# Modulation rows in four column tiles, set among the x transposes and inside the first projections

## What is computed

```python
silu_c = jax.nn.silu(c)
silu_cc = jax.nn.silu(c_ctx)
for l in range(DEPTH):
    mod_l = silu_c @ w_mod[l] + b_mod[l]
    mod_c = silu_cc @ w_mod[l] + b_mod[l]
    sh_l, sc_l, g_l = jnp.split(mod_l, 3, axis=-1)
    sh_c, sc_c, g_c = jnp.split(mod_c, 3, axis=-1)
    h_l = rmsnorm(x, norm_g[l]) * (1 + sc_l[:, None]) + sh_l[:, None]
    h_c = rmsnorm(ctx, norm_g[l]) * (1 + sc_c) + sh_c
```

## Time and profile before

| | us |
|---|---|
| median of 3 runs | 3099.61 (3099.58 to 3099.64) |
| the profiled execution | 3102.97 |
| its span, first to last instruction | 3101.2 |
| TensorE busy | 2782.8 |
| VectorE busy | 1442.6 |
| ScalarE busy | 1193.2 |
| mean granted TensorE clock | 0.962 |

### The profile page before, as it was taken

How to read it: one execution, slowest core, us unless ns; L and a number is a source line. 1 busy time by engine, 2 the same in 40 slices (tenths; PEclk the granted TensorE clock), 3 DMA queues, 4 the chain that set the end, 5 groups by cost and what they waited for, 6 DMA issues and landing times. The chain is left out here.

```text
span 3101.2 us, 40301 instructions
## 1 busy us (share of the span) xinstructions
PE 2782.8 (90%) x15627; PEld 2034.4 (66%) x15627; DVE 1442.6 (47%) x2485; ACT 1193.2 (38%) x2290; POOL 141.1 (5%) x235
## 2 busy tenths in 40 slices
PE   6899999898997989998998989999898989995667
PEld 1535675466664878897776868878333877885656
DVE  1202022455554661246787552431577546348752
ACT  1400122344444342215665442221567547224542
POOL 0000000000000000000000000000000010005410
PEclk9799999999998999999999999999999999998889
DMA  7150001000000121110000222010100221010002
GB/s 283 41 185 21 16 14 43 28 1 1 1 15 21 65 72 41 42 42 29 1 2 1 96 82 82 1 55 27 41 1 21 77 77 48 28 56 27 1 34 82
DMA packets 72094, 139.44 MB, mean 45 GB/s; under 512 B 2681, under 2 KB 31762, under 8 KB 71778
## 3 DMA queue, kind: packets, MB, share of 16 engines
q1 hardware_dynamic: 59056, 92.67, 8.6%
q0 software_dynamic: 12608, 44.13, 3.9%
q10 hardware_dynamic: 242, 0.07, 0.0%
HBM read 120.08 MB, written 16.78 MB: 44 GB/s over the span
## 5 line engine op out<-in xcount | busy, mean ns | idle before, releaser
L163 ACT ACTIVATE WORK<-PS 128x512 f32<-128x512 f32 (+6 forms) x421 | 205.1, 487 | 849.2 <-PE PS L702 290.1
L163 DVE TENSOR_REDUCE SM<-PS 128x2 f32<-128x1024 f32 (+2 forms) x192 | 201.1, 1047 | 157.7 <-PE PS L986 119.3
L734 PE MATMUL PS<-BASE,WORK 128*128 128x128 f32 (+1 forms) x1278 | 198.3, 289 | 73.7 <-DVE WORK L163 57.4
L163 DVE COPY WORK<-PS 128x512 f32<-128x512 f32 (+2 forms) x135 | 84.7, 627 | 360.9 <-PEq L760 157.3
L802 PE MATMUL PS<-WORK_R,HT_R 128*128 128x512 f32 x544 | 217.7, 400 | 20.6 <-DVE W_R L163 19.6
L734 PEld LDWEIGHTS PS<-BASE,WORK 128*128 128x128 f32 (+1 forms) x1278 | 149.3, 145 | 120.4 <-DVE WORK L163 55.7
L702 PE MATMUL PS<-HT_R,W_R 128*128 128x512 f32 x576 | 225.9, 392 | 0.0
L803 PE MATMUL PS<-WORK_R,MIXT_R 128*128 128x512 f32 x544 | 215.2, 395 | 0.0
L804 PE MATMUL PS<-W_R,HT_R 128*128 128x512 f32 x544 | 214.9, 395 | 0.0
L163 ACT ACTIVATE HT<-PS 128x512 f32<-128x512 f32 (+8 forms) x232 | 125.5, 541 | 230.0 <-PE PS L734 118.7
L681 PE MATMUL PS<-HT,W 128*128 128x512 f32 (+1 forms) x576 | 209.0, 526 | 0.3 <-PE PS L681 0.3
(11 more groups left out here) (235 smaller groups left out, 5449.2 us busy)
## 6 DMA issues: line engine op xcount, KB each, us to landing
W<-in_w_mod SPq DMA_DIRECT2D x12, 2048.0 KB, 7.9
x_scratch<-WORK POOLq DMA_DIRECT2D x24, 512.0 KB, 2.9
WORK<-x_scratch POOLq DMA_DIRECT2D x24, 512.0 KB, 3.6
W<-in_odd_w_in SPq DMA_DIRECT2D x12, 1024.0 KB, 5.2
W<-in_o_w_in SPq DMA_DIRECT2D x10, 1024.0 KB, 5.3
W<-in_even_w_in SPq DMA_DIRECT2D x5, 2048.0 KB, 7.8
WORK<-in_x POOLq DMA_DIRECT2D x16, 512.0 KB, 3.9
W<-in_e_w_in SPq DMA_DIRECT2D x3, 2048.0 KB, 9.0
```

The costliest lines, as they stand in the source:

```text
L163: self.last = Signalled(self, issue(*args, **kwargs))
L734: last = nc.tensor.transpose(bank[0:m, n * P:n * P + a.shape[0]], a, IDENT[0:a.shape[0], 0:a.shape[0]])
```

## The change

- *Column tiles.* SC is widened to 32 columns for each k (two used, the others zero). Product k of a row writes partitions 32(k mod 4) to 32(k mod 4) + 31 of the bank, so four partial sums of two k each arise. VectorE copies the whole bank of 128 partitions to MROW. The four instructions that make columns are now products with MROW stationary and ROW_SUM (128 x 2, built from the identity) moving, which add the four partial sums too.
- *Order.* Of layer 0 only rows 0 to 3 (shift and scale) stand ahead of f_gate, after x tiles 3, 5, 7 and 9. Rows 4 and 5 of layer 0 and all six of layer 1 are placed behind units 4, 7, 10 of f_gate and 1, 4, 6, 8, 10 of f_in, their columns one unit later. Their weights don't pass through W: POOL loads each into one 2 MB buffer, LATE_MOD, in MIXT, the first when f_gate's first unit is done, each further one when the row before is done.
- *x tiles.* Each of the ten has its own buffer (FIRST_X) and is loaded at once; the table TABL is loaded behind them. The evictions are plain copies of a bank of 128 x 512. Scale and shift are applied afterwards in place in HT, group by group, by ScalarE (blocks 0 to 3) and VectorE (4 to 7), and f_gate waits for its group.
- *SP* starts its loads without waiting for the constants.

```diff
-        MROW = work(16384, 1024)
+        MROW = [work(16384, 512), work(16896, 512)]
+        SC = work(17408, 256).rearrange("p (k c) -> p k c", k=KT)
+        ROW_SUM = SM[:, 90:92]
+        FIRST_X = [work(o, 1024) for o in (0, 1024, 2048, 3072, 6144, 7168, 10368, 11392, 12416, 13440)]
...
-        for m in range(6):
+        for m in range(4):
             add(f"mod0_{m}", rows_by_tile(mod_w[0], 512 * m, 512 * m + 512))
         add("f_gate", rows_by_tile(e_in, 512, 1024))
-        for m in range(6):
-            add(f"mod1_{m}", rows_by_tile(mod_w[1], 512 * m, 512 * m + 512))
...
+        mod_after = {3: 0, 5: 1, 7: 2, 9: 3}
+        late_mods = [(0, 4), (0, 5)] + [(1, m) for m in range(6)]
+        late_mod_after = {("f_gate", u): n for n, u in enumerate((4, 7, 10))}
+        late_mod_after.update({("f_in", u): 3 + n for n, u in enumerate((1, 4, 6, 8, 10))})
+        LATE_MOD = MIXT[:, 4:8, :].rearrange("p k c -> p (k c)")[:, 0:WSLOT].rearrange("p (k n) -> p k n", k=KT)
...
+            def mod_rows(l, m, w):
+
+                bank = open_unit(pe, ("mod", l, m), "dve")
+                for k in range(KT):
+                    r = 32 * (k % 4)
+                    last = mm(bank[r:r + 32, :], SC[:, k, :], w[:, k, :], start=k < 4, stop=k >= 4, skip_group_check=True)
+                finish_unit(last)
+
+            def mod_columns(l, m):
+
+                landed(pe, ("mod", l, m))
+                bank = open_unit(pe, ("modt", l, m), "dve")
+                for f in range(4):
+                    last = mm(bank[:, 2 * f:2 * f + 2], MROW[m % 2][:, f * P:(f + 1) * P], ROW_SUM, start=True, stop=True)
+                finish_unit(last)
+
+            def late_mod(name, u):
+
+                if (name, u) in late_mod_after:
+                    n = late_mod_after[name, u]
+                    pe.wait_ge(mod_in, 16 * (n + 1))
+                    mod_rows(*late_mods[n], LATE_MOD)
+                elif (name, u - 1) in late_mod_after:
+                    mod_columns(*late_mods[late_mod_after[name, u - 1]])
...
+            pe.wait_ge(silu_ready, 1)
+            for i in range(NT):
+                x_transposes(0, i)
+                if i in mod_after:
+                    name = f"mod0_{mod_after[i]}"
+                    mod_rows(0, mod_after[i], weights(pe, name))
+                    pe.wait_ge(unit_ready, len(by_index))
+                    end_chunk(name)
+                if i - 1 in mod_after:
+                    mod_columns(0, mod_after[i - 1])
+            mod_columns(0, 3)
...
@@ ScalarE @@
+                if b == 0:
+                    f(HTv[:, 0:4, c], heads4(bank), ACT.Copy).then_inc(ev["act"], 1)
+                    return
...
             boundary(0)
+            from_dve()
+            for g, (c0, c1) in enumerate(TG):
+                for q in range(4):
+                    ins = f(HTv[:, q, c0:c1], HTv[:, q, c0:c1], ACT.Identity,
+                            scale=ASC[:, 0, q, g == 0:(g == 0) + 1], bias=MOD[:, 0, q, g == 0:(g == 0) + 1])
+                ins.then_inc(h_scaled["act"], 1)
...
@@ VectorE @@
+            for i in range(NT + 2):
+                if i < NT:
+                    dve.wait_ge(first_x_in[i], 16)
+                    norm_rows(0, i)
+                if i < 2:
+                    continue
+                x_evict(0, i - 2)
+                if i - 2 in mod_after:
+                    mod_rows(0, mod_after[i - 2])
+                if i - 3 in mod_after:
+                    mod_columns(0, mod_after[i - 3])
...
@@ POOL and SP @@
-            dma(TABL[:, :], A["t_tabs"][0]).then_inc(tab_in, 16)
...
+            for i in range(NT):
+                dma(FIRST_X[i], rows_of(0, i, old)).then_inc(first_x_in[i], 16)
+            dma(TABL[:, :], A["t_tabs"][0]).then_inc(tab_in, 16)
+            pe_read(pool, ("f_gate", 0, 0))
+            for n, (l, m) in enumerate(late_mods):
+                if n:
+                    pe_read(pool, ("mod",) + late_mods[n - 1])
+                dma(LATE_MOD, rows_by_tile(mod_w[l], 512 * m, 512 * m + 512)).then_inc(mod_in, 16)
...
-            sp.wait_ge(const_in, 48)
-            sp.wait_ge(rows_in, 16 * 13)
```

More of the change, by code:

```diff
@@ L242, in build @@
         w_used = sem("w_used")
+        first_x_in = [sem(f"first_x_in{i}") for i in range(NT)]
+        mod_in = sem("mod_in")
+        sc_zero = sem("sc_zero")
+        h_scaled = {"act": sem("h_scaled_act"), "dve": sem("h_scaled_dve")}
         x_in = [sem(f"x_in{i}") for i in range(2)]
@@ L485, in build @@
         bound_at = {k: n for n, k in enumerate(bounds)}
+        rms_of = lambda n: SM[:, 2 + n % 2:3 + n % 2] if bounds[n][0] else SMX[:, n:n + 1]
+        x_loads = lambda n: (n - NT) // 2 + 1
         closes = {1: 1, 2: 2, 3: 4, 4: 6}
@@ L887, in _ @@
             gate("f_gate")
[L888 removed]
             w = weights(pe, "f_in")
[L890 removed]
+            for g, (c0, c1) in enumerate(TG):
                 for f in range(4):
                     project_t(("f_in", f, c0), w, f * P, c0, c1, "act" if f % 2 else "dve")
+                    late_mod("f_in", 4 * g + f)
             pe.wait_ge(unit_ready, len(by_index))
@@ L1423, in norm_stat @@
                 if bounds[n][0] == 0:
-                    act.wait_ge(x_in[n % 2], 16 * (n // 2 + 1))
+                    act.wait_ge(first_x_in[n], 16)
                 else:
                     from_dve()
-                link(f(JUNK_OF[bounds[n][0]], XIN[n % 2], ACT.Square, accum_out=SM[:, n % 2:n % 2 + 1]))
-                give(f(SM[:, 2 + n % 2:3 + n % 2], SM[:, n % 2:n % 2 + 1], ACT.Sqrt, scale=1.0 / D, bias=EPSC[:, :]))
+                x = XIN[n % 2] if bounds[n][0] else FIRST_X[n]
+                link(f(JUNK_OF[bounds[n][0]], x, ACT.Square, accum_out=SM[:, n % 2:n % 2 + 1]))
+                give(f(rms_of(n), SM[:, n % 2:n % 2 + 1], ACT.Sqrt, scale=1.0 / D, bias=EPSC[:, :]))
             def x_evict(b, i):
@@ L1871, in _, with mod_rows @@
             dve.wait_ge(ev["dve"], 1)
[L1873 to L1885, removed]
-                g0 = VA["norm_g"] + 8 * l
-                link(v.scalar_tensor_tensor(ASC[:, l, :, :], MOD[:, l, 8:16, :], 1.0,
-                                            VC[:, g0:g0 + 8].unsqueeze(2).to_broadcast([P, 8, 2]), ALU.add, ALU.mult))
+            def mod_rows(l, m):
+                if (l, m) in late_mods[2:]:
+                    pe_read(dve, ("modt",) + late_mods[late_mods.index((l, m)) - 2])
+                elif m >= 2:
+                    pe_read(dve, ("modt", 0, m - 2))
+                bank = take(dve, ("mod", l, m), "dve")
+                v.tensor_copy(MROW[m % 2], bank).then_inc(ev["dve"], 1)
@@ L2077, in row_max @@
                 return run
[L2080 to L2085, removed]
+            for i in range(NT + 2):
[9 more added lines that the diff above has]
+                    mod_columns(0, mod_after[i - 3])
+            mod_columns(0, 3)
+            give(scales(0))
+            for g, (c0, c1) in enumerate(TG):
+                for q in range(4, KT):
+                    ins = v.tensor_scalar(HTv[:, q, c0:c1], HTv[:, q, c0:c1], ASC[:, 0, q, g == 0:(g == 0) + 1],
+                                          MOD[:, 0, q, g == 0:(g == 0) + 1], ALU.mult, ALU.add)
+                ins.then_inc(h_scaled["dve"], 1)
+            for u in range(12):
+                late_mod("f_gate", u)
+            for g, (c0, c1) in enumerate(TG):
+                for q in range(4):
+                    if q % 2 == 0:
+                        copy_unit(("f_in", q, c0), UT[:, q, c0:c1], c1 - c0)
+                    late_mod("f_in", 4 * g + q)
+            landed(dve, ("modt", 1, 5))
+            link(scales(1))
             for c0, c1 in TG:
```

79 lines of the change are left out of this document (36 added, 43 removed).

## The result

The changed kernel takes **3022.11 us** (median of 4 runs, 3019.23 to 3024.24) where the kernel before took 3099.62 in the same comparison: ratio 0.9747, 95% interval 0.973 to 0.9764. The forecast was 3021, the range 3006 to 3043. The profiled execution took 3022.27 us with a span of 3020.2 (3102.97 and 3101.2 before).

What follows compares the result with a forecast made beforehand. TensorE, busy for 90% of the span, was taken as the bound. Gains of 51.6 us (part A) and 25.7 (part B), together 77.3, gave 3022.3 from the median, 3021 with SP's earlier start; range 3006 to 3043.

Steps and rivals of the forecast that it cites:

- Part A: Everything up to f_gate's start, at 104.64 us before: f_gate was to start at 53, a gain of 51.6 us.
- When it starts: TensorE's first x transposes, behind constants, small loads and first scaling: 18.7 us, with 2 us added for later landing.
- The groups: After the first four tiles, three groups of two tiles, one row and one set of columns: 6.3 us each.
- The last row and the tail: Between the groups and f_gate: 2.8 us for the fourth row, 4 for copy, columns, add, scale factors and scaling.
- The DMA sum: Loads up to f_gate's weights, 16.6 MB: 41 to 51 us plus 2 of latency, a floor of about 44.
- The column tiles: Modulation rows on TensorE: four tiles side by side, 1.7 us a row plus 0.3 for two mode changes, 2.0.
- The columns: The four products that turn a row into columns: 0.5 us, or 1.0 at half clock.
- Part B: From f_gate to the end of f_in: layer 1's modulation stage leaves (46.5 us), eight late rows cost 20.8; gain 25.7.
- 1.2 GHz in the tile stage: Rival: the x tile stage stays at half clock, f_gate starts at 62.7, total 3030.7 us; chance 0.17.
- The start slips: Rival: the thirteen small loads land near 20 us rather than 13, 7 us more, total 3028 to 3031; chance 0.06.
- The single buffer: Rival: late rows wait for 2 MB loads through one buffer; at 26 us a load the gain is gone; chance 0.04.
- Tiles by two or by one: Two rivals on rows: two tiles at a time, 3.5 us, total 3039, chance 0.09; one, 7.0 us, 3077, 0.04.

Runs made afterwards that it cites:

- the first experiment: The changed kernel with SP waiting again for the constants and the small loads before its own loads: 3021.68 us against 3022.11.
- the late load: The changed kernel with POOL issuing each late load one unit later, when the columns of the row before are done: 3039.02 us against 3022.11.

## Why the prediction was right

**Part A** was to end at 53 and ended at 50.82. *When it starts:* 18.7 was said, 18.97 it was; the small loads landed at 13.15, the 2 us more that I had added to 10.92. *The first four tiles* were to end at 27.3 and ended at 25.3: the first three sped up on the way (24 records in 4.24 us), and the fourth took 1.09, full speed. (The granted clock reads 1.00 in these rows from the start, so the speed-up is read from the durations.) *The groups* of two tiles, a row and columns: three in 18.6 us (25.26 to 43.85), 6.2 each for my 6.3. That is luck in good part. The middle between 4.5 and 8.9 was a choice rather than a derivation, and no group took it: they took 7.0, 6.6 and 5.0. Nor were three engines equally full; ScalarE was busy for less than half of the last group's stretch. TensorE was not always at full clock (0.66 from 31 to 36 us) and waited 1.76 us for VectorE at the first columns, where the copy of the bank stands behind the next tile's scaling. *The last row and the tail* were put at 2.8 and 4 and took 1.9 and 5.05. Together: 2.0 us less up to the first row, 0.3 in the groups, 0.9 in the last row, 1.05 more in the tail. The step that was too small is the scaling of the first group: I took 0.38 us for a pass over 256 columns from a row of an eviction without scale and bias vectors; with them, and in place, it took ScalarE 0.60. The last line is of the kernel before:

```profile
L163 ACT ACTIVATE HT<-HT,MOD,ASC 128x256 f32<-128x256 f32 x4 | 2.4, 599 | 4.2 <-DVE ASC L163 4.1
L163 DVE TENSOR_SCALAR HT<-HT,ASC,MOD 128x256 f32<-128x256 f32 x4 | 1.7, 413 | 0.1
...
L163 ACT ACTIVATE HT<-PS,MOD,ASC 128x128 f32<-128x128 f32 x40 | 18.3, 458 | 1.9
```

This line could have told it: with both vectors a pass over 128 columns took 0.46 us there, from PSUM. By the earlier trace rows 256 columns more cost 0.21, so 128 more cost 0.11, which makes 0.57 for 256. The vectors are thus the larger part of the miss, and reading SBUF instead of PSUM at most a small one.

*The DMA sum* put a floor of 44 us under f_gate's weights. They were issued at 35.98 and landed 12.3 us later, at 48.3, with the engines full from 10 us on: right in kind, 4 us short, and 2.5 us ahead of f_gate's start.

**The column tiles.** 2.0 us a row with its two changes of mode was said, 1.86 measured from the row's start to the next unit, and the bounds 3.5 and 7.0 were then met closely by two groups and one (3.63 and 7.05). The 1.86 are 0.10 above a quarter of an unbroken row (7.03), 0.15 above the 1.71 I had reckoned with. The unit ahead of a row takes longer too: 7.04 us from 198.21 to 205.25, where its 16 records unbroken are 6.90 (f_in's 192 records before, worth 160 of that width, took 69.01). The Trainium skill ("TensorEngine Tiling (Array Packing)", Key Properties) names a drain at a change of tiling mode. The trace agrees in that 0.25 to 0.3 us are lost around a row with its two changes, as the sum had it; that the loss is the drain isn't shown.

**The columns** were mis-sized: 0.5 us said, 0.81 us from their start to the next unit. I had halved a tile of eight transposes, 1.97 us at half clock, this line of before:

```profile
77.43 1.97 PE L734 MATMUL PS<-BASE,WORK 128*128 128x128 f32 x8 [5.63 <-DVE WORK L163]
```

But a transpose is one record and an fp32 product two: the four products are eight records (x8 at 83.08), where half a tile is four.

**Part B** was to gain 25.7 and gained 22.3: from f_gate's start to m_gate's it took 186.8 us before (104.64 to 291.44) and takes 164.5 (50.82 to 215.33). A late row with its columns costs 2.9 us and not 2.6:

```profile
188.57 1.92 PE L768 MATMUL PS<-MIXT,WORK 128*32 128x512 f32 x16
...
198.21 7.11 PE L700 MATMUL PS<-HT,W 128*128 128x512 f32 x16
205.25 1.92 PE L768 MATMUL PS<-MIXT,WORK 128*32 128x512 f32 x16
```

From row to row go 16.68 us, of which two units alone are 13.8. Eight times 2.9 is 23, 2.2 more than the 20.8 of the sum, most of it in the columns. The other 1.2 us are f_gate's start at half clock, which costs 2.6 us and cost 2.0 before (71.00 against 69.01), and 0.4 us at the end of f_gate and of f_in each (131.42, 215.33), where TensorE waits for VectorE's add; before there was one gap of 0.3 (291.44).

**The total.** Both parts together give 76.1 for the 77.3 of the sum: part A gained 2.2 more than said (53.8 for 51.6) and part B 3.4 less. That the forecast of 3021 is within 1.1 us of the median is therefore luck of two misses with opposite signs, beside a sum whose terms mostly held; its last microsecond, for SP's early start, had nothing behind it (the first experiment). The spans differ by 81.0, 4.9 more than the two parts. This comes far behind the change: L1166 first ran at 1935.2 before and its counterpart at 1858.2 after, 77.0 apart; L1235 at 2186.1 and 2107.1, 79.0. The medians differ by only 77.5, the profiled execution of before was 3.4 above its median, and runs of the changed kernel differ by 5, so I take it for a difference of the two executions and no part of the change; it wasn't tested.

**The rivals.** *1.2 GHz in the tile stage:* happened for stretches only. (Its terms add up to 62.5 and 3030.5, not 62.7 and 3030.7.) The Trainium skill's rule that transposes don't count for the clock ("TensorE: Matmul & The Clock Gate", Part 4) disagrees with these runs: after transposes alone eight of them took 1.09 us and the next row 1.92, both full speed (24.24 and 25.26). The clock fell only in or right behind stretches in which TensorE also stood idle; whether the idle time alone let it fall wasn't separated. *The start slips:* by the 2 us foreseen. *The single buffer:* loads took 8.6 us, and delaying them showed waits of the size that the formula gives; it also showed that a wait costs clock beyond its length, which the formula lacked. *Tiles by two or by one:* four groups took about the quarter, and the pair of the earlier trace rows had been good evidence for it.

## What to carry to other kernels

A product with few stationary columns can be cut along its contraction into column groups, and four fp32 groups then take about a quarter of the time (1.92 us for 7.05); but the weights must come as fast, so short rows pay only when spread among other work (29 us alone, 77 with the order). Place such pieces in the engine's gaps, and look at the queue's slots too: the same rows behind the tiles instead of between them cost 9 us, of which the trace shows only 1.6 as a wait for weights, beside gaps left empty and a lower clock. And look at what follows a pause: here 3.1 us ahead of a long run of products cost 2.6 us more behind it, which useless products in the pause gave back, while waits of 1.9 us in a stretch otherwise full (the late load) cost nothing more.

## What was not expected of the hardware

- With a pause of about 3.1 us ahead of f_gate its first 80 records took 22.8 to 23.9 us, in all eight profiles of kernels that have it; with three useless products in the pause they took 20.92, in all three that had them.
- With three 2 MB loads and ten of 512 KB in flight, the small constants of POOL's queue reached VectorE at 10.29 us (5.92 before), and the thirteen tiny ones of ScalarE's queue at 13.15; with SP held back the latter came at 10.70.
- An in-place pass of ScalarE over 128x256 in SBUF with scale and bias vectors took 0.60 us, one from PSUM without them 0.38; with them, from PSUM, 128 columns took 0.46.
